# Second mixer of a hybrid decoder step: two VectorE copies become ScalarE writes from PSUM, and eight kept rows are multiplied in the output projection stage

## The reference, cut to what matters

```python
def odd_mixer(u, li, h0, conv0):
    g, xr = jnp.split(u @ w_in_odd[o], 2, axis=-1)
    x_ext = jnp.concatenate([conv0.astype(xr.dtype), xr], axis=1)
    xc = causal_conv(x_ext, conv_w[o], conv_b[o]).astype(f32)
    ...
    h = linear_scan(a, b, h0.astype(f32))
    y = (h.astype(u.dtype) * jax.nn.gelu(g)) @ w_out_odd[o]
    return y, h[:, -1], x_ext[:, -(CONV_W - 1):]
```

## Time and profile before

| what | value |
|---|---|
| median of 3 runs | 1480.92 us (1480.09 to 1483.02) |
| the profiled execution, its own time | 1479.19 us |
| its span in the profile | 1477.5 us |
| TensorE busy | 1357.9 us, 92% of the span |
| VectorE busy | 1020.0 us, 69% |
| ScalarE busy | 693.8 us, 47% |
| GpSimd busy | 367.8 us, 25% |

### The profile page before, as it was taken

One profiled execution on the slowest core, in us unless ns is written; L12 is line 12 of the kernel. 1 busy time (PEld: TensorE's weight loads), 2 busy tenths in 40 slices (PEclk: granted clock), 3 DMA queues, 4 the chain that ended last, 5 costly groups with the idle time before them and its releaser, 6 DMA issues.

```text
span 1477.5 us, 30333 instructions
## 1 busy us (share of the span) xinstructions
PE 1357.9 (92%) x11788; PEld 1297.8 (88%) x11788; DVE 1020.0 (69%) x1623; ACT 693.8 (47%) x1162; POOL 367.8 (25%) x347
## 2 busy tenths in 40 slices
PE   4999987889897999999999999997988999999996
PEld 3899966666697999999999889897987999999995
DVE  4533258754566999449984888897687983699646
ACT  1311152334433566426762446884435762467534
POOL 2000031122125310121103538463650101210054
PEclk8999998899998999999999999998998999999999
DMA  9732278667912343366523312222622524665211
GB/s 311 232 91 81 87 258 278 222 222 262 292 41 75 58 109 93 99 139 139 123 76 110 106 44 80 93 69 59 169 43 66 125 76 120 126 139 116 81 40 58
DMA packets 233573, 185.02 MB, mean 125 GB/s; under 512 B 9687, under 2 KB 203996, under 8 KB 233316
## 3 DMA queue, kind: packets, MB, share of 16 engines
q1 hardware_dynamic: 208448, 160.13, 35.2%
q0 software_dynamic: 24864, 23.20, 8.3%
q10 hardware_dynamic: 140, 0.09, 0.0%
HBM read 177.83 MB, written 5.63 MB: 124 GB/s over the span
## 4 chain that ended last, share of the span: by engine, by line
PE 50%; DVE 15%; ACT 3%; issue 1%; POOL 0%; DVEq 0%; ACTq 0%; POOLq 0%
PE ps L3313 26%; PE ps L3154 16%; PE ps L3163 4%; PE ps L3183 3%; DVE gn L2459 2%; DVE wlo L2225 2%; DVE UL L2466 1%; DVE xc L2712 1%; DVE rstd L2432 1%; ACT whi L1295 1%; DVE xc L2747 1%; DVE xc L2746 1%; DVE tL L2551 1%; DVE wlo L2233 1%; DVE qT L2732 0%
## 5 line engine op out<-in xcount | busy, mean ns | idle before, releaser
L1308 ACT ACTIVATE whi<-raw 128x512 fp32r<-128x512 f32 x266 | 168.4, 633 | 109.0 <-DVE raw L2243 47.0
L1295 ACT ACTIVATE whi<-raw 128x2048 fp32r<-128x2048 f32 (+3 forms) x66 | 105.1, 1593 | 235.6 <-PE ps L3154 177.4
L2233 DVE TENSOR_TENSOR wlo<-raw,whi 128x512 fp32r<-128x512 f32 x266 | 186.3, 700 | 14.6 <-ACT whi L1308 4.9
L3313 PE MATMUL ps<-UH,whi 128*128 128x260 f32 x608 | 172.7, 284 | 0.2 <-DVE hb L2568 0.2
L3313 PE MATMUL ps<-UL,whi 128*128 128x260 f32 x608 | 172.8, 284 | 0.0
L3313 PE MATMUL ps<-UH,wlo 128*128 128x260 f32 x608 | 172.2, 283 | 0.0
L2225 DVE TENSOR_TENSOR wlo<-raw,whi 128x2048 fp32r<-128x2048 f32 (+3 forms) x66 | 136.2, 2063 | 42.1 <-ACT whi L1295 40.1
L3154 PE MATMUL ps<-UH,whi 128*128 128x260 f32 x688 | 140.2, 285 | 11.5 <-DVE wlo L2225 11.4
L3154 PE MATMUL ps<-UH,wlo 128*128 128x260 f32 x688 | 139.4, 284 | 0.0
L3154 PE MATMUL ps<-UL,whi 128*128 128x260 f32 x688 | 139.3, 284 | 0.0
L3313 PE MATMUL ps<-tH,whi 128*128 128x260 f32 x456 | 130.6, 286 | 6.9 <-ACT ps L1495 6.9
(11 more groups left out here) (551 smaller groups left out, 3500.3 us busy)
## 6 DMA issues: line engine op xcount, KB each, us to landing
raw<-in_w_ada SPq DMA_DIRECT2D x96, 512.0 KB, 6.7
raw<-in_w_ffn_in SPq DMA_DIRECT2D x88, 512.0 KB, 5.1
raw<-in_w_in_even SPq DMA_DIRECT2D x24, 512.0 KB, 4.8
raw<-in_w_ffn_out SPq DMA_DIRECT2D x32, 384.0 KB, 4.1
raw<-in_w_ffn_out SPq DMA_DIRECT2D x32, 320.0 KB, 3.3
raw<-in_w_in_odd SPq DMA_DIRECT2D x20, 512.0 KB, 4.5
raw<-in_w_ffn_in POOLq DMA_DIRECT2D x38, 256.0 KB, 4.7
raw<-in_w_out_odd SPq DMA_DIRECT2D x16, 320.0 KB, 3.6
```

Source lines behind the costliest of these rows:

```text
L1295: ins = nc.scalar.activation(whi[w][:, 0:f], raw[c % NRAW][:, 0:f], ACT.Identity)
L1308: nc.scalar.activation(seven_block(b)[0], seven_source(c, b), ACT.Identity).then_inc(seven_hi, 1)
L2233: v.tensor_tensor(low, seven_source(c, b), high.bitcast(F32), ALU.subtract).then_inc(seven_lo, 1)
L3313: ins = T.matmul(out, wt[:, k], x, start=(b in (0, 1) and k == 0 and wt is wh and x is xh), stop=(k == 3 and wt is wl_), skip_group_check= ...
```

## The change

The three state columns and the eight sample columns of `OS` are written by ScalarE straight from PSUM in `conv_input`; the buffer `xrS` and the two VectorE copies go. All eight `keep_normalized` calls move in GpSimd's order from between the blocks to behind the ten gate products, ahead of the output stores. The eight `keep` calls move in ScalarE's order: two stand ahead of the output projection's loop, the other six inside it. The residuals of `r = 2` wait for their own tile of `x_ready`, as those of odd `r` already did.

```diff
@@ GpSimd, second mixer
                             low_xc(2 * b + 2)
                             low_xc(2 * b + 3)
-                            keep_normalized(2 * b)
-                            keep_normalized(2 * b + 1)
                         gated_inputs(2 * b)
                         gated_inputs(2 * b + 1)
...
                         pool.tensor_tensor(xc[:, t], xc[:, t], gate_buf(t)[:], ALU.mult).then_inc(y_ready, 1)
                         settled(pool, y_ready)
+                    for t in range(KD):
+                        keep_normalized(t)
                     pool.wait_ge(out_ready, 2)
@@ ScalarE, conv_input(t)
-                nc.scalar.activation(xrS[:, t].rearrange("p (a b) -> p a b", a=2), ps(g)[:, :, HALF:HT], ACT.Identity)
+                nc.scalar.activation(OS[:, t, 3:11].rearrange("p (a b) -> p a b", a=2), ps(g)[:, :, HALF:HT], ACT.Identity)
+                nc.scalar.activation(OS[:, t, 0:3], ps(g)[:, 1, HALF - 3:HALF], ACT.Identity)
@@ ScalarE, order of the second mixer (pairs 0-1, 2-3, 4-5 and 6-7 go)
             high_xc(5)
-            keep(1, 0)
-            keep(1, 1)
             conv_input(6)
...
             high_y(8)
             high_y(9)
+            keep(1, 0)
+            keep(1, 1)
             s = st["oout"]
             for c in range(s.n - 2):
+                keep(1, c + 2)
                 if c >= 1:
                     squares(2, c - 1)
                 hi(s.c0 + c + 2)
@@ VectorE, residual
-                if r % 2 == 1:
+                if r >= 1:
                     dve.wait_ge(x_ready, 8 * (r - 1) + t + 1)
-                elif t == 0 and r >= 1:
-                    dve.wait_ge(x_ready, 8 * r)
@@ VectorE, half_residual
                 if hf == 0:
+                    if r == 2:
+                        dve.wait_ge(x_ready, 8 * (r - 1) + t + 1)
                     dve.wait_ge(half_filled, 3 * r + i + 1)
@@ VectorE, convolve(t), and behind convolve(9)
                 dve.wait_ge(cv0, t + 1)
-                v.tensor_copy(OS[:, t, 0:3], xr[:, t, SEQ:SEQ + 3])
...
-            link(v.tensor_copy(OS[:, :, 3:11], xrS[:]))
```

More of the change, by code:

```diff
@@ L306, in trunk @@
         psig = sb("psig", [P, 1])
-        xrS = sb("xrS", [P, KR, NS])
         pgt = sb("pgt", [P, 16], I32)
@@ L1686, in _ @@
             high_xc(7)
-            keep(1, 2)
-            keep(1, 3)
             conv_input(8)
@@ L1704, in _ @@
             hi(p0 + 12)
-            keep(1, 4)
-            keep(1, 5)
             gates(4)
@@ L1734, in _ @@
             high_y(3)
-            keep(1, 6)
-            keep(1, 7)
             gelu(6)
```

## The result

| | before | after |
|---|---|---|
| median | 1480.04 us | 1484.76 us |
| range of the runs | 1477.38 to 1487.24 (14 runs) | 1482.62 to 1490.66 (14 runs) |
| profiled execution, its own time | 1479.19 us | 1483.66 us |
| its span | 1477.5 us | 1482.0 us |

The kernel became slower: the ratio of after to before is 1.0029, with a 95% interval of 1.0018 to 1.0040. That is 4.3 us (2.7 to 5.9) where +4.0 was forecast; the median lies 0.1 us from the predicted 1484.9. So close a hit is luck: runs of one kernel lie 8 to 10 us apart, and the forecast counted from a median of 1480.92 where the 14 runs have 1480.04.

A forecast was written before the change was run, and what follows sets the result against it. TensorE was taken to bound most of the span, VectorE the second mixer. Terms -1.0 + 5.0 = +4.0 us took the profiled 1479.19 to 1483.2; the median, 1.73 above, gave 1484.9, range 1479.5 to 1488.0.

The forecast's parts named there:

- The tail, +5.0: Start of the output projection: eight late GpSimd multiplications delay VectorE's low parts, so the first chunk ends 5.0 us later.
- The turn of 1.70 us: Before the output projection: VectorE and GpSimd alternate, one turn of each costing 1.70 us, 0.97 more for a YL.
- The front, -1.0: Early in the second mixer: the multiplication pair at 889.01 leaves, gaining 1.2 us; with added copies -1.0 when scans end.
- The weight split: ScalarE's split near 891 us: it becomes what is late, its low part starting at 891.0 and taking 2.30.
- The added ScalarE copies, 0.06 each: Ten small ScalarE copies in the mixer: 0.06 us each, three or four on the chain, cost 0.2 us.
- The VectorE copies, 0: In `convolve`: ten small copies leave for 0 gain (bounds 0 and 8.2 us), the 80-column copy 0, at most 1.2.
- The new waits of the residuals: In the output projection: each residual waits on its own tile, ready before TensorE's whole first chunk; cost 0.
- the moved scalings: ScalarE's eight scalings leave the mixer for 0 gain and fit into ScalarE's waits in the output projection.
- Rival 1: Before the output projection: the late products hide, VectorE's steps do not lengthen, only -1.0 is left: 1479.9; chance 0.14.
- rival 2: Output projection: only its start slips, the last YL does not matter, end moves +2.0: 1482.9; chance 0.13.
- rival 3: Through the mixer: VectorE is the bound throughout, so the kernel gets faster, -5.0: 1475.9; chance 0.10.
- rival 4: Before the output projection: no overlap in a pair, 2.1 us instead of 1.70, +7 in all: 1487.9; chance 0.05.

The follow-up runs named there:

- e3_late: Kernel after, but GpSimd waits for the last low part YL before the eight multiplications; 1480.62 us, ratio to before 1.0009.
- e6_half: Kernel after, but four of the eight multiplications stand in the middle of the mixer, four behind the gate products; 1492.91 us in one execution.
- e2_move: Kernel after with the two VectorE copies put back, so only the multiplications and scalings move; 1485.79 us, ratio to before 1.0047.
- e5_first: Against e3_late, only the first two multiplications go back to where the kernel before had them; 1482.12 us, ratio to before 0.9997.
- e1_copies: Kernel after with multiplications and scalings put back, so only the VectorE copies are replaced by ScalarE writes; 1479.81 us, ratio to before 0.9998.
- e11_scalings: Kernel after with all eight GpSimd multiplications at their old places, copies replaced and scalings moved; 1481.27 us in one execution.
- e9_again: The kernel before, unchanged, profiled once more; 1482.67 us in one execution.

## Why the prediction was right, step by step

- **The tail, +5.0: right, +5.17 in T.** The turn of 1.70 us was the right price (1.67 to 1.70 for the seven `YL` that it was laid on, 2.46 for the weight's low part where 2.55 was taken); the wait ahead of the start grew by 2.68 and the waits inside the chunk were 1.60, where 3.0 and 2 were given. The end hangs on the last `YL`: counted from the first one it ends 7.80 us later (19.12 instead of 11.32), where 7.85 was forecast, and the six matmuls behind it take 0.99, where 0.72 was. `e3_late` removes the cost, `e6_half` shows its two parts, `e2_move` that nothing else is needed.
- **The front, -1.0: the way was right, the size short, the step behind it right only in part.** A is 0.91 shorter, but B is 0.11 longer, and 0.13 is lost just ahead of A (15.54 us from TensorE's start at 857.37 in the kernel after, 15.41 from 859.29 before), so about 0.7 of the 1.0 is there. The weight split did become late, as VectorE's timeline of the kernel after shows, only earlier than the 891.0 forecast, because this execution's stage began 1.8 us earlier:

```profile
889.15 2.29 DVE L2220 TENSOR_TENSOR wlo<-raw,whi 128x2048 fp32r<-128x2048 f32 x1 [0.88 <-ACT whi L1294]
...
1036.55 0.17 DVE L2381 TENSOR_TENSOR stmp<-ps,modT 128x8 f32<-128x8 f32 x1 [2.66 <-PE ps L3147]
```

But the low part ends at 891.44 and TensorE starts at 891.87: it waits for `rT`, the sigmoid that empties its PSUM buffer. ScalarE's timeline of the kernel after has it, with the added copies:

```profile
886.00 0.17 ACT L1618 ACTIVATE OS<-ps 128x8 f32<-128x8 f32 x1
886.06 0.18 ACT L1619 ACTIVATE OS<-ps 128x3 f32<-128x3 f32 x1
886.11 0.80 ACT L1620 ACTIVATE xc<-ps,OT 128x520 f32<-128x520 f32 x1
...
889.74 1.28 ACT L1631 ACT_TABLE_LOAD   x1
891.03 1.42 ACT L1631 ACTIVATE rT<-ps,OT 128x520 f32<-128x520 f32 x2
...
1011.59 0.82 ACT L1387 ACTIVATE xT<-xT,lnA 128x520 f32<-128x520 f32 x1 [1.06 <-POOL xT L990]
```

  The table load of 1.28 us ahead of `rT` had been on no list. What it leaves of the pair's gain is 0.71 (A of `e5_first` less that of the kernel after), where the prediction had 1.2 and at least 0.9.
- **The added ScalarE copies, 0.06 each: right.** The starts above are 0.06 and 0.05 apart, and `e1_copies` with all of them measures 0.9998. The 0.13 ahead of A and the 0.11 in B stand in it too (15.55 and 64.87): together the 0.2 that was forecast, against 0.19 that A gains there (19.68).
- **The VectorE copies, 0: right.** `e1_copies` takes them out for no gain. Most of their 8.2 us went where the prediction put them, into the add behind them: the ten adds take 1.5 us before and 8.0 in `e1_copies`, whose products stand as before, and the groups by line of the kernel after show them too (columns as in the earlier trace rows):

```profile
L2704 DVE TENSOR_TENSOR xc<-xc,tS 128x8 f32<-128x8 f32 x10 | 7.3, 732 | 2.9 <-ACT xc L1620 2.6
```

- **The new waits of the residuals and the moved scalings, 0: right.** The residual at 1036.55 waits 2.66 us for TensorE's `ps`, as in the earlier trace rows, not for ScalarE, whose first scaling began at 1011.59; `e11_scalings` moves the scalings alone and keeps W and T (8.71 and 15.13, before 8.93 and 15.00).
- **Rivals.** Rival 1 (the products hide) and rival 2 (only the start slips) fall by the rows of 1.7 and the wait of 1.27 ahead of the last six matmuls; rival 3 (VectorE bound throughout) by `e1_copies` and by A, which gave 0.9 and not 5; rival 4 by 1.70 instead of 2.1.
- **Missed: the clock behind the 2.98 us wait.** It puts 1.2 to 2.3 us into some executions (C of 22.96 after, 23.99 in `e9_again`, 21.72 otherwise). The prediction did not name it. Whether it belongs in the scatter or, at least in part, in the sum stays open, since seven of seven profiles with the products moved show it and one of five without; the measured 4.3 (2.7 to 5.9) fits the stages' 4.4 without it and their 5.65 with it, so its nearness to +4.0 does not decide.

## What to carry to other kernels

A timeline in which one kind of instruction has two lengths (0.73 and 1.70 us here) names a partner on another engine; find the partner, and its count times the difference is the price of whatever is moved into or out of that company. An engine's idle time is a free place only if the work put there fits into it and meets no step on the path: by the stages, the same eight products cost 5 us beside the low parts, 1.5 in the middle, where four cost nothing, and nothing behind the last low part. (The whole time of the kernel with eight in the middle, 4.6 us above before, is more than its stages explain.) A queue's last wait is worth undoing only after the next one behind it has been read.

## What the runs showed of the hardware

- VectorE and GpSimd, both with two SBUF operands, alternate instruction by instruction: 1.67 to 1.70 us for a pair whose halves take 0.71 and 1.30 by themselves (1.30 is a GpSimd product of the earlier trace rows that goes ahead of VectorE's step; the median of the 24 products with `rstd` in the kernel before is 1.32), 0.3 less than their sum, steady over eight pairs. GpSimd memsets (4.66 us for eight) leave VectorE's 0.71 as it is.
- Behind the same 3.0 us wait the granted clock of TensorE fell to the 1.2 GHz level in one execution and stayed at 2.4 GHz in another of the same kernel (0.50 and 1.00); 24 matmuls took 5.58 us after that fall, 4.54 after the one in the kernel after, and 3.16 without.
